# Half of the low parts of 38 weight blocks formed by POOL instead of DVE

## The chip, the cores and the metric

The kernel runs on one core of a Trainium2 chip. The time is device microseconds of one launch: the median of the runs, which are compared with the runs of the kernel before on the same chip.

## What is computed

A model of two blocks of two layers each, 256 tokens of width 1024, all in 32-bit floats. The change lies in the first block, whose layer has a differential attention, an attention over the 64 best keys of an index score (the sparse attention), gates, and 32 experts:

```python
h = x @ w_in
dq, dkk, dv, sq, sk, sv, iq, ik, iw, ga, gb = jnp.split(h, points, axis=-1)
...
lam = jnp.exp(jnp.sum(lp[0] * lp[1])) - jnp.exp(jnp.sum(lp[2] * lp[3])) + lam_init
ya = diff_attention(dq, dkk, dv, lam)
ya = (rms_norm(ya, subln_g) * (1.0 - lam_init)).reshape(B, S, DIFF_WIDTH)
...
topk = min(TOPK_MAX, S // 4)
yb = dsa_attention(sq, sk, sv, iq, ik, iw, topk)
merged = jax.nn.sigmoid(ga) * (ya @ w_bd) + jax.nn.sigmoid(gb) * (yb @ w_bs)
return merged @ w_o
```

The second block (latent attention, block attention, retention, a squared-ReLU MLP) and the experts stay as they are.

## The kernel before

**Split products.** A dense product is made of three matmuls on high and low parts (`mm3`, line 1149): high by high, high by low, low by high. So each dense weight block, up to 128 x 2048 words, 1 MB, is split after it has landed in a ring buffer: ACT rounds it into the high part `WSh` in two halves (line 2126, signal `hi_done`, one count for each half), and DVE subtracts high from the landed block into the low part `WSl`, again in two halves (line 1516, signal `lo_done`). There are 218 such blocks of different widths; 38 of them, all 2048 words wide, are touched by the change. There are three landing buffers (`RING`) and three pairs of high and low parts (`PAIRS`).

**Order.** A planner (`Plan`) writes one list of steps, and each of the engines walks the same list and does its part of each step, in that order. PE, ACT, DVE, POOL and SP's queue are each in order; they meet only in semaphores. `take` puts the fetch and the split of a block into the list two blocks ahead of the matmuls that use it (`ahead`, line 183). The split of block i+3 may begin when PE has read block i, since it goes into the same pair; the fetch of block i+3 waits in SP's queue until the split of block i is done (line 1126).

**The stretch of the change.** In layer 0 it begins behind the iq projections. In the list stand: the small late loads that POOL issues (line 2380 and on, among them the tokens `X`), the rotary tables on DVE, POOL's scaling of `X` by a constant (line 2389, behind the landing of `X`), the rotary step of iq. Then come the four blocks of the sq and sk projections (blocks 4 to 7), the index scores, two blocks each of dq, dk and dv with the steps of the top-64 search between them (DVE, lines 1647 to 1657), the transposes, the differential attention with one gate block in each of its waits, and the sparse attention with sv, the branch product and two more gate blocks among its steps. A round of softmax goes PE (scores), DVE (mask and row maximum, lines 1670 to 1674), ACT (exponentials, line 2182), DVE (lines 1681 to 1698), PE (transposes of the probabilities, line 1276). In the list, the split of a block stands between those DVE steps. Layer 1 has the same stretch with no loads and no scaling in front of it.

**POOL before.** In this stretch it issues the late loads, scales `X`, and takes two tiny powers for the norm of the differential attention (line 2374, one for each half of the tokens), for which DVE waits.

Of the kernel before, what the change touches and what calls it, by code (L numbers as in the profile page):

```python
# [7 lines left out]
F32 = mybir.dt.float32  # L8
# [3 lines left out]
ALU = mybir.AluOpType  # L12
# [33 lines left out]
PAIRS = 3  # L46
# [54 lines left out]
class Plan:  # L101
# [3 lines left out]
    def __init__(self, order):  # L105
# [9 lines left out]
        self.limit = 3  # L115
        self.also = {}

    def add(self, kind, **fields):
# [71 lines left out]
    def prepare(self, j, spec):  # L190
# [7 lines left out]
        if not self.is_raw(at) and j not in self.split_no:  # L198
            m = self.split_no[j] = len(self.split_block)
            self.split_block.append(j)  # L200
            self.add("split", i=j, m=m, n=width(at), buffer=self.fetched[j])
            self.give_back(j)

# [148 lines left out]
    def first_layer(self, l):  # L352
# [11 lines left out]
        if l == 0:  # L364
            self.add("scale_x", l=l)
        self.add("rope", name="iq", l=l)
        self.columns("w_in", "sq", l, W1["sq"], 1024, src)
        if l == 0:
# [28 lines left out]
        def diff_out():  # L397
# [3 lines left out]
            self.todo.extend(self.gates("w_in", l, "gb", W1["gb"], src))  # L401
        self.attend("dsa", l, 8, (1, 2, 1), diff_out, pre=1)
        for n, name in enumerate(("A0", "A1")):
            self.lend(name, ("pe", "turned", "DT", l, 3), at=RING + n)
# [341 lines left out]
def build(nc, plan, table, wts, rows, cols, consts, pos, x0, x0T, pT, out):  # L746

    ctx = ExitStack()
    with ctx:
# [7 lines left out]
        done = {"pe": pe_done, "act": act_done, "dve": dve_done, "pool": pool_done}  # L757
        hi_done, lo_done = signal("hi_done"), signal("lo_done")
        landed = {n: signal(f"landed_{n}", 16) for n in (*(f"ring{i}" for i in range(RING)), "PT", "H", "V0", "V1", "YA", "YB", "A0", "A1", "SC", "W0", "W1")}
# [357 lines left out]
        def sync_program(e):  # L1117
            sp = Waiter(e)
            e.dma_start(XR[:, 4:8, :], x0T[:, 4:8, :]).then_inc(*xt_in[1].inc(("all",)))
            for s in plan.steps:  # L1120
                l = s.l
                if s.kind == "fetch":
                    if isinstance(s.before, tuple):
                        sp.wait_ge(done[s.before[0]], *s.before[1:])
                    elif s.before in plan.split_no:
                        sp.wait_ge(lo_done, "block", s.before)
                    elif s.before is not None:
                        sp.wait_ge(pe_done, "read", s.before)
# [14 lines left out]
        def tensor_program(e):  # L1143
# [17 lines left out]
            def bank_free(u):  # L1161
                if u >= 4:
                    pe.wait_ge(emptied(u - 4), "bank", u - 4)

            def scp_free(use):
                if use:
                    pe.wait_ge(freed("scp", use - 1), "scp", use - 1)
# [6 lines left out]
            for s in plan.steps:  # L1174
                l, i, u = s.l, s.i, s.u
                if s.kind == "wide":
                    lhs = MGS[s.h] if s.name == "w_out" else [x_[:, 4 * s.h:4 * s.h + 4, :] for x_ in XT]
                    w = [w_[:, 0:4 * s.n].rearrange("p (k n) -> p k n", k=4) for w_ in WS[plan.split_no[i] % PAIRS]]
                    pe.wait_ge(lo_done, "block", i)
                    for t in range(T):  # L1180
# [11 lines left out]
                elif s.kind in ("gate", "mlp_up", "ret_gate"):  # L1192
                    w = halves(i)
                    pe.wait_ge(lo_done, "block", i)
                    bank_free(u)
# [5 lines left out]
                elif s.kind == "branch":  # L1201
                    w = halves(i)
                    pe.wait_ge(lo_done, "block", i)
                    for m in range(2):
# [97 lines left out]
                elif s.kind in ("ple", "q_up"):  # L1302
                    w = halves(i)
                    pe.wait_ge(lo_done, "block", i)
                    if s.kind == "ple":
# [13 lines left out]
                elif s.kind == "kv_up":  # L1319
                    w = halves(i)  # L1320
                    pe.wait_ge(lo_done, "block", i)
                    bank_free(u)
# [109 lines left out]
                elif s.kind == "mlp_down":  # L1432
                    w = halves(i)
                    pe.wait_ge(lo_done, "block", i)
                    pe.wait_ge(dve_done, "mlp_up", l, s.q, s.c)
# [24 lines left out]
        def vector_program(e):  # L1460
# [43 lines left out]
            for s in plan.steps:  # L1504
                l, i, u, t = s.l, s.i, s.u, s.t
                if s.kind == "split":
                    hi, lo = WS[s.m % PAIRS]
                    buf = buffers[s.buffer]
                    for k in range(2):
                        c = slice(k * (s.n // 2), s.n // 2 if k == 0 else s.n)  # L1510
# [855 lines left out]
        def gpsimd_program(e):  # L2366
# [9 lines left out]
            for s in plan.steps:  # L2376
                l, t = s.l, s.t
                if s.kind == "late_loads":
                    pool.wait_ge(act_done, "iq", 0, 1)
# [118 lines left out]
```

## Time and profile before

| | |
|---|---|
| median of 3 runs | 1873.83 us (1873.68 to 1877.28) |
| the profiled execution | 1872.17 us |
| its span, first to last instruction | 1870.1 us |
| PE busy | 1795.5 us (96%) |
| DVE busy | 1116.6 us (60%) |
| ACT busy | 833.7 us (45%) |
| POOL busy | 69.6 us (4%) |
| stretch of the change in layer 0 | about 30 to 165 us |
| stretch of the change in layer 1 | about 510 to 650 us |

All times of rows are microseconds from the start of the span of the profiled execution. PE's busy time counts the instructions in flight, so the idle time before an instruction (in square brackets in the order-of-time view, with the instruction that ended it) tells more than a share of busy time. In the view of stretches, the number behind POOL's is the granted TensorE clock: 1.00 is 2.4 GHz, 0.50 is 1.2 GHz, a value between is a mean of the two over the stretch.

### The profile page before, as it was taken

What the parts mean: (1) busy time and instruction counts of PE and PEld (TensorE: products, weight loads), DVE (VectorE), ACT (ScalarE), POOL (GpSimd) and SP (SyncE); (2) the same over time, 40 slices, a digit from 0 to 9 for tenths busy, and PEclk for the clock granted to TensorE, in tenths of its full rate; (3) what the DMA queues carried; (4) which work ended last, traced back from release to release, by engine and by line L of the source; (5) the groups of instructions that cost most, each with busy time, mean ns of one, the idle gap of its engine ahead of it and who ended that gap; (6) DMA issues with size and microseconds to landing.
All of it is one profiled execution on the core that took longest, in us unless ns stands there. A gap on an engine that the chain in (4) does not pass through costs nothing.

```text
span 1870.1 us, 29654 instructions
## 1 busy us (share of the span) xinstructions
PE 1795.5 (96%) x12304; PEld 1480.8 (79%) x12304; DVE 1116.6 (60%) x2049; ACT 833.7 (45%) x1436; POOL 69.6 (4%) x76
## 2 busy tenths in 40 slices
PE   7999999999899999999989999999999999999998
PEld 6788885555678899555548899989998889989997
DVE  5876773233678867433248666774447577675445
ACT  5545442232445444323226465344445555344442
POOL 2000000000000000000001000001001000000011
PEclk9999999999999999999999999999999999999999
DMA  7426669999653385899984434445554533355552
GB/s 290 158 91 240 229 238 411 421 420 420 242 185 113 135 324 203 346 420 421 421 341 168 159 114 157 158 165 197 182 185 153 203 132 120 135 197 180 182 196 73
DMA packets 61052, 426.64 MB, mean 228 GB/s; under 512 B 6960, under 2 KB 7104, under 8 KB 11888
## 3 DMA queue, kind: packets, MB, share of 16 engines
q1 hardware_dynamic: 59760, 421.65, 59.6%
q8 instruction: 100, 1.64, 0.3%
q0 software_dynamic: 432, 1.82, 0.3%
q10 hardware_dynamic: 720, 1.19, 0.2%
q14 instruction: 40, 0.33, 0.0%
HBM read 423.59 MB, written 1.05 MB: 227 GB/s over the span
## 4 chain that ended last, share of the span: by engine, by line
PE 81%; DVE 14%; ACT 4%; issue 1%; POOL 1%; DMA 0%; DVEq 0%; ACTq 0%; POOLq 0%
PE bank L1147 63%; PE scp L1147 14%; DVE WSl L1516 4%; ACT SC L2182 1%; PE bank L1390 1%; DVE sm L1672 1%; ACT WSh L2126 1%; PE bank L1249 1%; PE bank L1276 1%; DVE scp L1670 1%; POOL sm L2374 1%; PE bank L1223 1%; DVE sm L1473 0%; DVE XTl L1781 0%; DVE SC L1684 0%
## 5 line engine op out<-in xcount | busy, mean ns | idle before, releaser
L1516 DVE TENSOR_TENSOR WSl<-ring,WSh 128x1024 fp32r<-128x1024 f32 (+3 forms) x404 | 459.7, 1181 | 179.6 <-ACT WSh L2126 179.4
L2126 ACT CAST WSh<-ring 128x1024 fp32r<-128x1024 f32 (+3 forms) x404 | 390.2, 1020 | 157.9 <-PE scp L1147 88.0
L1147 PE MATMUL bank<-XTh,WSh 128*128 128x256 f32 x1216 | 348.2, 286 | 4.3 <-DVE GT L1796 2.5
L1147 PE MATMUL bank<-XTl,WSh 128*128 128x256 f32 x1216 | 344.7, 283 | 0.0
L1147 PE MATMUL bank<-XTh,WSl 128*128 128x256 f32 x1216 | 344.5, 283 | 0.0
L1147 PEld LDWEIGHTS bank<-XTh,WSh 128*128 128x128 f32 x1216 | 234.0, 192 | 7.5 <-DVE WSl L1516 4.1
L1147 PEld LDWEIGHTS bank<-XTl,WSh 128*128 128x128 f32 x1216 | 234.1, 192 | 0.2
L1147 PEld LDWEIGHTS bank<-XTh,WSl 128*128 128x128 f32 x1216 | 233.9, 192 | 0.0
L1147 PE MATMUL bank<-WSh,XTh 128*128 128x512 f32 (+4 forms) x544 | 203.1, 373 | 12.4 <-DVE WSl L1516 10.7
L1147 PE MATMUL bank<-WSh,XTl 128*128 128x512 f32 (+4 forms) x544 | 201.0, 370 | 0.0
L1147 PE MATMUL bank<-WSl,XTh 128*128 128x512 f32 (+4 forms) x544 | 200.8, 369 | 0.0
L2013 DVE SCALAR_TENSOR_TENSOR TMP<-TMP,bank 128x128 f32<-128x128 f32 x64 | 18.4, 288 | 279.1 <-ACT TMP L2312 279.1
L1147 PE MATMUL scp<-WSh,FA 128*128 128x512 f32 x512 | 159.3, 389 | 0.0
L1147 PEld LDWEIGHTS bank<-WSh,XTh 128*128 128x128 f32 x544 | 104.6, 192 | 28.2 <-DVE WSl L1516 10.9
L1147 PE MATMUL bank<-FA,WSh 128*128 128x256 f32 x640 | 117.6, 286 | 0.1
L2316 ACT COPY WSF<-bank 128x256 f32<-128x256 f32 x64 | 23.8, 372 | 210.2 <-PE bank L1147 210.2
L1147 PEld LDWEIGHTS bank<-WSh,XTl 128*128 128x128 f32 x544 | 104.4, 192 | 14.1
L1147 PEld LDWEIGHTS bank<-WSl,XTh 128*128 128x128 f32 x544 | 104.7, 192 | 13.4
L1147 PEld LDWEIGHTS scp<-WSh,FA 128*128 128x128 f32 x512 | 96.1, 188 | 19.8
L1147 PEld LDWEIGHTS bank<-FA,WSh 128*128 128x128 f32 x640 | 100.5, 193 | 1.9 <-issue 1.9
L1147 PE MATMUL scp<-WSl,FA 128*128 128x512 f32 x256 | 99.7, 389 | 0.0
L1147 PE MATMUL bank<-WSh,FA 128*128 128x512 f32 (+1 forms) x336 | 94.7, 364 | 0.0
(310 smaller groups left out, 2666.9 us busy)
## 6 DMA issues: line engine op xcount, KB each, us to landing
ring<-wts SPq DMA_DIRECT2D x222, 1024.0 KB, 4.8
A<-wts SPq DMA_DIRECT2D x64, 1024.0 KB, 14.2
V<-wts SPq DMA_DIRECT2D x30, 1024.0 KB, 15.5
WSF<-wts SPq DMA_DIRECT2D x24, 1024.0 KB, 16.0
SC<-wts SPq DMA_DIRECT2D x16, 1024.0 KB, 15.5
PT<-wts SPq DMA_DIRECT2D x14, 1024.0 KB, 16.5
H<-wts SPq DMA_DIRECT2D x12, 1024.0 KB, 16.0
ring<-wts SPq DMA_DIRECT2D x8, 584.0 KB, 5.3
```

The costliest lines, as they stand in the source:

```text
L1147: return nc.tensor.matmul(dst, lhsT, rhs, start=start, stop=stop)
L1223: last = nc.tensor.transpose(bank[u % 4][0:s.w, j * P:(j + 1) * P], src, ident)
L1249: last = nc.tensor.transpose(bank[u % 4][:, j * P:(j + 1) * P], src(t, c), ident)
L1276: last = nc.tensor.transpose(bank[u % 4][:, (j - s.first) * P:(j - s.first + 1) * P], p_at(j // nk)[:, j % nk * P:(j % nk + 1) * P], ident)
L1390: last = nc.tensor.transpose(bank[u % 4][:, f * P:(f + 1) * P], SE[s.e % 2][:, f * P:(f + 1) * P], ident)
L1516: nc.vector.tensor_tensor(lo[:, c], buf[:, c], hi[:, c].bitcast(F32), ALU.subtract).then_inc(*lo_done.inc(("block", i)))
L1670: nc.vector.tensor_tensor(v, v, mask.unsqueeze(1).broadcast_to([P, 4, kl - m0]), ALU.add).then_inc(*dve_done.inc())
L1672: nc.vector.tensor_reduce(mx[:, h], scp[:, h, 0:kl], AX.X, ALU.max).then_inc(*dve_done.inc())
L2126: nc.scalar.copy(hi[:, c], buffers[s.buffer][:, c]).then_inc(*hi_done.inc(("half", i, k)))
L2182: ins = nc.scalar.activation(SC[:, h, 0:kl], scp[:, h, 0:kl], ACT.Exp, bias=nb[t][:, h:h + 1], scale=SCALE[s.name], accum_out=zs[t][:, h:h ...
L2316: nc.scalar.copy(SE[s.e % 2], bank[u % 4][:, 0:DE]).then_inc(*act_done.inc(("bank", u), ("SE", l, s.e)))
L2374: nc.gpsimd.tensor_tensor(var, var, const("nhalf")[:, 0:groups], ALU.pow).then_inc(*pool_done.inc(("pow", *name)))
```

## The change

The planner has a flag, `aid`, true from the sq projections to the end of the sparse attention in each layer. Blocks whose split step is written while it is true are "aided": 19 in each layer (6 to 24 in layer 0), the first of them the third sq and sk block, since its split is written when the first is taken. For an aided block DVE subtracts the first half alone; POOL waits for the second high half, and for the pair to be free, subtracts the second half, and counts on a semaphore of its own, `lo2_done`. PE, and SP's queue before it loads over the landed block, wait for both.

```diff
@@ prepare
             self.add("split", i=j, m=m, n=width(at), buffer=self.fetched[j])
+            if self.aid:
+                self.aided.add(j)
             self.give_back(j)
@@ first_layer
         self.add("rope", name="iq", l=l)
+        self.aid = True
         self.columns("w_in", "sq", l, W1["sq"], 1024, src)
...
         self.attend("dsa", l, 8, (1, 2, 1), diff_out, pre=1)
+        self.aid = False
@@ SP
                         sp.wait_ge(lo_done, "block", s.before)
+                        if s.before in plan.aided:
+                            sp.wait_ge(lo2_done, "block", s.before)
@@ PE
+            def split_ready(i):
+                pe.wait_ge(lo_done, "block", i)
+                if i in plan.aided:
+                    pe.wait_ge(lo2_done, "block", i)
...
-                    pe.wait_ge(lo_done, "block", i)
+                    split_ready(i)
@@ DVE
-                    for k in range(2):
+                    for k in range(1 if i in plan.aided else 2):
@@ POOL
             for s in plan.steps:
                 l, t = s.l, s.t
-                if s.kind == "late_loads":
+                if s.kind == "split" and s.i in plan.aided:
+                    hi, lo = WS[s.m % PAIRS]
+                    c = slice(s.n // 2, s.n)
+                    pool.wait_ge(hi_done, "half", s.i, 1)
+                    if blocks_free(s.m) is not None:
+                        pool.wait_ge(pe_done, "read", blocks_free(s.m))
+                    nc.gpsimd.tensor_tensor(lo[:, c], buffers[s.buffer][:, c], hi[:, c].bitcast(F32), ALU.subtract).then_inc(
+                        *lo2_done.inc(("block", s.i)))
+                elif s.kind == "late_loads":
```

## Rows read from the trace of the kernel before

**Rows 1.** The page: busy us of each engine, share of the span, instructions

```profile
PE 1795.5 (96%) x12304; PEld 1480.8 (79%) x12304; DVE 1116.6 (60%) x2049; ACT 833.7 (45%) x1436; POOL 69.6 (4%) x76
```

**Rows 2.** PE in order of time, layer 0: start, us, instruction, [idle before <- who ended it]

```profile
91.50 0.36 PE L1147 MATMUL bank<-XTh,WSh 128*128 128x256 f32 x1 [0.80 <-DVE A L1715]
...
99.99 0.38 PE L1147 MATMUL scp<-A 64*128 64x128 f32 x2 [0.77 <-ACT A L2190]
...
119.02 1.07 PE L1276 MATMUL bank<-CST,SC 128*128 128x128 f32 x4 [1.82 <-DVE SC L1698]
120.58 1.11 PE L1276 MATMUL bank<-CST,SC 128*128 128x128 f32 x4 [0.49 <-DVE SC L1698]
...
146.93 0.65 PE L1276 MATMUL bank<-CST,SC 128*128 128x128 f32 x4 [2.22 <-DVE SC L1684]
...
163.41 1.25 PE L1276 MATMUL bank<-CST,SC 128*128 128x128 f32 x8 [0.57 <-DVE H L1796]
```

**Rows 3.** PE in order of time, layer 1

```profile
537.03 1.16 PE L1147 MATMUL scp<-A 64*128 64x128 f32 x16 [1.69 <-DVE A L1715]
...
583.39 1.16 PE L1147 MATMUL scp<-A 64*128 64x128 f32 x16 [0.88 <-DVE A L1715]
...
602.43 0.66 PE L1276 MATMUL bank<-CST,SC 128*128 128x128 f32 x4 [1.84 <-DVE SC L1698]
604.00 1.12 PE L1276 MATMUL bank<-CST,SC 128*128 128x128 f32 x4 [0.91 <-DVE SC L1698]
...
630.91 1.93 PE L1276 MATMUL bank<-CST,SC 128*128 128x128 f32 x8 [2.22 <-DVE SC L1684]
```

**Rows 4.** Stretches: PE, PEld, DVE, ACT, POOL busy, granted clock, DMA share, GB/s

```profile
118.00:124.00 6.00, 4.49 (x26) 4.09 (x27) 4.77 (x19) 4.00 (x6) 0.80 (x1) 0.72 0.00 0
602.00:608.00 6.00, 4.66 (x26) 4.42 (x27) 4.63 (x20) 3.62 (x6) 1.02 (x1) 0.72 0.00 0
630.00:638.00 8.00, 6.21 (x35) 5.27 (x36) 6.62 (x11) 2.38 (x9) 0.00 (x0) 0.57 0.43 144
490.00:498.00 8.00, 2.99 (x14) 3.02 (x15) 5.64 (x14) 3.09 (x5) 1.04 (x2) 0.57 0.25 81
144.00:152.00 8.00, 4.86 (x47) 3.82 (x44) 7.86 (x11) 2.75 (x9) 0.00 (x0) 1.00 0.64 246
88.00:94.00 6.00, 5.20 (x42) 4.79 (x41) 5.57 (x11) 3.66 (x5) 0.00 (x0) 1.00 0.85 311
```

**Rows 5.** DVE and ACT in order of time ahead of two of the waits

```profile
108.32 2.35 DVE L1516 TENSOR_TENSOR WSl<-ring,WSh 128x1024 fp32r<-128x1024 f32 x2
...
142.09 2.03 ACT L2126 CAST WSh<-ring 128x1024 fp32r<-128x1024 f32 x2
...
143.71 2.35 DVE L1516 TENSOR_TENSOR WSl<-ring,WSh 128x1024 fp32r<-128x1024 f32 x2
```

**Rows 6.** POOL by line, whole span: out<-in, forms, count | busy us, mean ns | idle before

```profile
L2419 POOL TENSOR_TENSOR TMP<-TMP 128x512 f32<-128x512 f32 x32 | 33.3, 1042 | 387.5 <-ACT TMP L2355 387.5
L2389 POOL TENSOR_SCALAR X<-X 128x2048 f32<-128x2048 f32 x1 | 8.9, 8852 | 8.2 <-DMA X<-x 8.2
```

**Rows 7.** The chain of waits: start, us, the matmuls of two projection blocks

```profile
53.85 11.15 PE bank L1147 x48
```

**Rows 8.** POOL, DVE and ACT in order of time around the first aided blocks

```profile
32.47 8.85 POOL L2389 TENSOR_SCALAR X<-X 128x2048 f32<-128x2048 f32 x1 [8.19 <-DMA X<-x]
...
31.46 4.62 DVE L1516 TENSOR_TENSOR WSl<-ring,WSh 128x1024 fp32r<-128x1024 f32 x4
39.05 2.75 DVE L1516 TENSOR_TENSOR WSl<-ring,WSh 128x1024 fp32r<-128x1024 f32 x2 [2.97 <-ACT WSh L2126]
...
32.10 2.00 ACT L2126 CAST WSh<-ring 128x1024 fp32r<-128x1024 f32 x2 [0.56 <-PE bank L1147]
37.49 0.60 ACT L2155 ACTIVATE A<-bank 128x512 f32<-128x512 f32 x1 [2.12 <-PE bank L1147]
```

**Rows 9.** PE in order of time at the longest idle time nearby

```profile
495.01 3.38 PE L1249 MATMUL bank<-CST,H 128*128 128x128 f32 x16 [5.24 <-ACT H L2275]
```

More of the change, by code:

```diff
@@ L116, in __init__ @@
         self.also = {}
+        self.aid, self.aided = False, set()
     def add(self, kind, **fields):
@@ L757, in build @@
         done = {"pe": pe_done, "act": act_done, "dve": dve_done, "pool": pool_done}
-        hi_done, lo_done = signal("hi_done"), signal("lo_done")
+        hi_done, lo_done, lo2_done = signal("hi_done"), signal("lo_done"), signal("lo2_done")
         landed = {n: signal(f"landed_{n}", 16) for n in (*(f"ring{i}" for i in range(RING)), "PT", "H", "V0", "V1", "YA", "YB", "A0", "A1", "SC", "W0", "W1")}
@@ L1193, in tensor_program @@
                     w = halves(i)
-                    pe.wait_ge(lo_done, "block", i)
+                    split_ready(i)
                     bank_free(u)
@@ L1202, in tensor_program @@
                     w = halves(i)
-                    pe.wait_ge(lo_done, "block", i)
+                    split_ready(i)
                     for m in range(2):
@@ L1303, in tensor_program @@
                     w = halves(i)
-                    pe.wait_ge(lo_done, "block", i)
+                    split_ready(i)
                     if s.kind == "ple":
@@ L1320, in tensor_program @@
                     w = halves(i)
-                    pe.wait_ge(lo_done, "block", i)
+                    split_ready(i)
                     bank_free(u)
@@ L1433, in tensor_program @@
                     w = halves(i)
-                    pe.wait_ge(lo_done, "block", i)
+                    split_ready(i)
                     pe.wait_ge(dve_done, "mlp_up", l, s.q, s.c)
```

## The prediction

> **What bounds the kernel now.** I read the page first. PE is busy for 96% of the span, DVE for 60%, ACT for 45%, POOL for 4% [rows 1]. So work moved from DVE to POOL pays only where PE stands idle, and that is read in the order-of-time view of PE, from its brackets. In the stretch of layer 0 PE is idle nine times between 66 and 165 us, and the longer ones end on DVE: 0.80 us on the eviction of a transpose, 1.82 and 0.49 on the last steps of a softmax, 2.22 on a normalised softmax, 0.57 on a product's eviction [rows 2]. In layer 1 it is 0.88, then 1.84 and 0.91, then 2.22 us [rows 3]. The 0.77 us before 99.99 ends on ACT [rows 2], and the 1.69 us before 537.03 ends on an eviction at the head of the stretch that no aided split stands before [rows 3]. The whole prize in idle time is thus under 10 us of 1872.
>
> A second prize stands in the view of stretches. Behind some of these waits the granted clock falls to 1.2 GHz: 0.72 as the mean of 118 to 124 us and of 602 to 608, 0.57 over 630 to 638; but behind the equal wait of 2.22 us at 146.93 it stays at 1.00 [rows 4]. With 1 minus the mean, times two, times the stretch, that is 3.4, 3.4 and 6.9 us at the lower level. Where PE works through them it loses half: less the idle time inside them 1.4, 1.6 and 3.0 us, 6.0 together.
>
> **The change part by part.**
>
> *Off DVE.* 19 halves a layer, 38 in all. A pair of 128x1024 subtractions takes 2.35 or 2.36 us where neither is held up [rows 5], so a single one some 1.2 and the second adds 1.14; 43 us leave DVE. What each wait gets of that:
> - At 91.50 and 583.39 six and eight aided splits stand ahead among the search steps, each 1.14 us less, so DVE is far ahead. Layer 0 gains its whole 0.80. In layer 1 the next late thing is ACT's eviction of the last transpose group, which costs 0.77 at the same kind of place in layer 0 [rows 2]; so it gains 0.88 - 0.77 = 0.11.
> - At 119.02 and 602.43 one split stands in the DVE chain between the two halves of the softmax (108.32 [rows 5]); the rest is mask, maximum, ACT's exponentials and the mix. Gain 1.14 in each layer, leaving 1.17 of 2.31 and 1.61 of 2.75.
> - At 146.93 and 630.91 two splits stand ahead, but DVE then waits for ACT: the high half of the second starts on ACT at 142.09 and is there at 143.1 (half of 2.03), DVE's half takes to 144.3, and reciprocal and product some 0.9 more, to 145.2 instead of 146.87 [rows 2, 5]. Gain 1.65 in each layer.
> - At 163.41 two splits stand ahead of 0.57: gain 0.57.
>
> Together 0.80 + 1.14 + 1.65 + 0.57 = 4.2 us in layer 0 and 0.11 + 1.14 + 1.65 = 2.9 in layer 1: **7.1 us**.
>
> *Clock.* The idle times behind which it fell shrink to about 0.6 us (0.7 and 0.5 at the mix; 2.22 - 1.65). The wait of 0.80 at 91.50 left it at 1.00 [rows 4]. I take the large one and one of the two small ones as gone, 3.0 + 1.6 = **4.6 us**; bounds 0 (the 1.00 behind 2.22 us shows that a wait's length alone does not decide it) and 6.0.
>
> *Onto POOL.* The nearest row is its product of two 128x512 tiles, 1042 ns [rows 6]; twice that is 2.08 us for 128x1024, and 38 of them are 79 us. PE takes 5.6 us for a block of the projections (11.15 for two [rows 7]) and the split is two blocks ahead, so in the steady run some 11 us lie over ACT's 2.0 and POOL's 2.1; only where POOL took 9 us for one would that cover be gone. SP's fetch of block i+3 waits for the later of the two parts of block i; it must land before PE has read i, which POOL's part precedes, so it keeps a block's time of cover: nothing. In POOL's queue the powers for the norm stand between splits. The split behind the first one starts at 124 us instead of when its high part is ready; DVE took it no sooner before. Nothing of POOL is due when a power is wanted: nothing, at most one subtraction, 2.08 us, in a layer.
>
> *The new wait.* POOL's first aided split (block 6) stands behind its scaling of X, which waits for X to land and runs from 32.47 to 41.32 us [rows 8]. Block 6 is due when PE ends block 5 at 37.4 (ACT evicts that product at 37.49 [rows 8]). Behind it on PE is everything; the third and fourth sq and sk blocks, the rotary step, the index scores and all of DVE's search follow from them, so this is not got back by the slack of later waits. How long it is depends on how long the scaling takes when DVE is not subtracting. In its 8.85 us DVE subtracts for 3.6 us at first and from 39.05 on, and the scaling ends while DVE still does [rows 8]; from 36.08 to 39.05 DVE is idle. Lower end: it advances only while DVE does not, needs some 3.5 to 4 us, and with two of the four halves gone (DVE free from 34.3 on: ACT's first half at 33.1 by the row of 32.10, and 1.2) ends at 38; block 6 then takes to 40.4, since DVE subtracts at 39.05 again. Stall 3.0 us. Upper end: 8.85 us is its own pace, and block 6 is ready at 43.4: 6.0 us. The lowest value I can build, no interference at all with the short pace, is 2.0. I take **3.0**: 8.85 us is 4.3 ns an element for one input, where two inputs cost 2.0 [rows 6], and the subtractions beside it are what differs. The clock may fall behind it: behind 5.24 us of idle time [rows 9] it is 0.57 over 490 to 498, with PE at work for the last 3.0 of them [rows 4], so **1.5**, bounds 0 and 1.5.
>
> *Beside each other.* Of DVE's pairs around the scaling, one took 2.75 instead of 2.36: 0.39 us paid in 8.85 us of POOL's work [rows 8], 0.09 for a POOL subtraction of 2.08. About ten of them stand in a chain that ends in a wait: **1.0 us**, bounds 0 and 3.9 (0.39 each).
>
> **Sum:** -7.1 - 4.6 + 3.0 + 1.5 + 1.0 = -6.2 us; the profiled execution took 1872.17, so 1866.0. The median stands 1.66 above that execution: **1867.7**. Its own bounds: 1862 (all clock, start 2.0, nothing paid) to 1875 (no clock, 3.0 + 1.5 + 3.9 paid).
>
> By the Trainium skill, GPSIMD Engine Reference, Engine selection, an elementwise operation with one input runs on GPSIMD "roughly" at line rate. For 2048 elements at its 1.2 GHz that is an estimate of 1.7 us, far under the 8.85 of the row, which it would put down to the subtractions beside it; by it the start would cost the 2.0 end, and the sum be -7.2.
>
> **The rivals.**
>
> *A. The scaling's own pace is 8.85 us.* For it: the row as it stands. Against: POOL's pace with two inputs. Stall 6.0: 1867.7 + 3.0 = 1870.7, within 0.2% of no change.
>
> *B. Other engines end the waits.* The round of a softmax goes through ACT's exponentials and its two halves of a high part, 2.0 us [rows 8], and one wait of layer 0 is ACT's. If the mix and the normalised softmax gain half of what I took (2.8 instead of 5.6) and no clock comes back: -4.3 + 5.5 = +1.2, 1875.0. No change that can be told.
>
> *C. POOL's subtraction holds DVE (the other side).* Place: each of DVE's operations with two inputs in SBUF, as its own halves, the mix and the rotary products, that comes while POOL reads. If it pays p for each POOL subtraction, DVE gains 1.14 - p. From p about 1.1 the idle times stay, the clock too, and the start is paid: 1878.3, slower. At the full 2.08 the six and eight splits before 91.50 and 583.39 add 0.94 each, and so do five or so behind them in each layer: 24 x 0.94 = 22, 1901. For it: nothing here but the 0.39. Against: three DVE halves started and ended at their usual 1.2 us inside the 8.85.
>
> The Trainium skill says, in SBUF — State Buffer, Who interferes with whom, that a DVE instruction with two SBUF inputs contends with a GpSimd instruction that reads SBUF, and that whichever starts first blocks the other for the whole instruction. By that, C is the outcome wherever POOL starts first. The row does not agree for a whole instruction: DVE's subtractions at 33.8 and 39.05 did not wait for the scaling to end [rows 8].
>
> **How the numbers follow.** Chances: forecast 0.42, A 0.20, B 0.18, C 0.20. A measurement of this kernel can tell about 0.2% (3.7 us) from no change, so faster means under 1870.1. Faster: nearly all of the forecast and a quarter of A, 0.46. Slower (over 1877.6): C and a little of B, 0.22. Same: 0.32. The range leaves out the strong half of C (0.1) and a tail below: 1861 to 1882.
>
> **What would show it.** POOL's subtraction at 2.1 us near idle DVE. PE's first idle time at 37.4 us, 3 us long, ended by POOL (6 for A), with the scaling of X ending near 38 (41.3 for A). The waits at the two mixes and normalised softmaxes down to about 0.6 each, those at 91.5 and 163.4 gone, the clock at 1.00 behind 630. In C, DVE's halves well over 1.2 us in the stretch. Wrong would be: PE waiting for `lo2_done` anywhere but at block 6; DVE's own durations unchanged and the idle times unchanged all the same (B).

## The result, and the profile after

The changed kernel is slower: 1896.47 us median (1895.12 to 1897.13, 4 runs) beside 1873.76 us of the kernel before (1873.61 to 1877.28, 4 runs), ratio 1.0116, 95% interval 1.0098 to 1.0133. I had predicted 1867.7 us, with a range of 1861 to 1882, and 0.22 for slower. The profiled execution took 1896.2 us, its span is 1894.1 us, 24.0 longer than before; the mean granted clock is 0.983, before 0.990. Executions of one kernel differ by themselves: those of the kernel before, over all runs of this document, took 1871.3 to 1877.5 us with a mean granted clock of 0.992 to 0.985, so what one profiled execution shows of the clock can be off by some us.

The page's busy times, to be read beside [rows 1]:

```profile
PE 1804.4 (95%) x12304; PEld 1488.1 (79%) x12304; DVE 1123.7 (59%) x2011; ACT 834.4 (44%) x1436; POOL 162.4 (9%) x114
```

DVE has lost 38 subtractions, 38 x 1.14 = 43.3 us by the prediction's own price, and yet it is busy for 7.1 us more than before, not for 1116.6 - 43.3 = 1073.3 us. Something adds 50.4 us to instructions that are themselves unchanged. That is the first thing to see in this case: it doesn't show as a wait but as duration.

POOL by line and form (busy us, mean ns of one, then the idle time before):

```profile
L2396 POOL TENSOR_TENSOR WSl<-ring,WSh 128x1024 fp32r<-128x1024 f32 x38 | 96.2, 2535 | 176.3 <-ACT WSh L2138 176.3
L2409 POOL TENSOR_SCALAR X<-X 128x2048 f32<-128x2048 f32 x1 | 5.5, 5516 | 8.1 <-DMA X<-x 8.1
```

Where nothing is in the way a subtraction takes 2.35 us on POOL, not 2.08 (98.97 below), and the mean is 2.54. The scaling of `X`, 8.85 us in [rows 6], is 5.52.

PE in order of time, the waits that answer to [rows 2] and [rows 3], and the new one at the start (columns as there):

```profile
39.93 0.77 PE L1154 MATMUL bank<-WSh,XTh 128*128 128x512 f32 x1 [2.91 <-issue]
...
100.93 0.36 PE L1154 MATMUL bank<-XTh,WSh 128*128 128x256 f32 x1 [4.55 <-DVE A L1727]
121.47 0.66 PE L1288 MATMUL bank<-CST,SC 128*128 128x128 f32 x4 [1.51 <-DVE SC L1710]
...
161.06 1.97 PE L1288 MATMUL bank<-CST,SC 128*128 128x128 f32 x8 [4.40 <-DVE SC L1696]
...
602.61 1.83 PE L1154 MATMUL scp<-A 64*128 64x128 f32 x16 [3.16 <-DVE A L1727]
652.94 1.97 PE L1288 MATMUL bank<-CST,SC 128*128 128x128 f32 x8 [4.39 <-DVE SC L1696]
```

The 0.80 us before the gate block's matmul has become 4.55, the 2.22 us before the transposes of the normalised softmax 4.40, the same one of layer 1 4.39 instead of 2.22, and the 0.88 before the scores 3.16. All of PE's waits of the layer-0 stretch are 21.0 us together (11.1 before) and those of layer 1 14.2 us (9.1 before): 15.0 more. The other 8.9 us of the 24.0 are PE busy longer (1804.4 against 1795.5) on the same 12304 instructions.

That part is the clock: it is 0.983 or 0.984 in all four executions of the change, under every one of the kernel before. Stretches of layer 0 (columns as in [rows 4]):

```profile
160.00:162.00 2.00, 0.94 (x5) 0.84 (x6) 1.78 (x3) 0.00 (x0) 0.46 (x1) 0.50 1.04 332
164.00:166.00 2.00, 2.00 (x17) 1.67 (x16) 1.93 (x4) 0.46 (x2) 0.00 (x0) 0.50 0.31 131
```

Behind the wait of 4.40 us the granted clock is 0.50, that is 1.2 GHz, through 166 us; behind the 2.22 us of the kernel before it had stayed at 1.00 [rows 4].

POOL and DVE in order of time, by pairs: a POOL subtraction, then the instructions of DVE beside it.

```profile
62.02 2.48 POOL L2396 TENSOR_TENSOR WSl<-ring,WSh 128x1024 fp32r<-128x1024 f32 x1 [10.26 <-ACT WSh L2138]
62.17 2.42 DVE L1659 TENSOR_SCALAR TMP<-PT,sm 128x128 f32<-128x128 f32 x1
...
91.37 2.50 POOL L2396 TENSOR_TENSOR WSl<-ring,WSh 128x1024 fp32r<-128x1024 f32 x1 [2.61 <-ACT WSh L2138]
90.79 0.42 DVE L1621 TENSOR_TENSOR TMP<-A,ropeb 128x256 f32<-128x256 f32 x1
91.52 2.63 DVE L1621 TENSOR_TENSOR TMP<-A,ropeb 128x256 f32<-128x256 f32 x1
...
98.97 2.35 POOL L2396 TENSOR_TENSOR WSl<-ring,WSh 128x1024 fp32r<-128x1024 f32 x1 [5.11 <-ACT WSh L2138]
99.24 0.43 DVE L1667 MAX8 sm<-TMP 128x8 f32<-128x256 f32 x1
99.78 0.41 DVE L1669 MATCH_REPLACE8 TMP<-sm,TMP 128x256 f32<-128x256 f32 x1
...
118.33 2.35 POOL L2396 TENSOR_TENSOR WSl<-ring,WSh 128x1024 fp32r<-128x1024 f32 x1 [17.01 <-ACT WSh L2138]
118.40 2.42 DVE L1710 SCALAR_TENSOR_TENSOR SC<-SC,sm 128x128 f32<-128x128 f32 x1
121.06 0.35 DVE L1710 SCALAR_TENSOR_TENSOR SC<-SC,sm 128x128 f32<-128x128 f32 x1
...
158.02 2.43 POOL L2396 TENSOR_TENSOR WSl<-ring,WSh 128x1024 fp32r<-128x1024 f32 x1 [0.90 <-ACT WSh L2138]
158.38 2.62 DVE L1696 TENSOR_TENSOR SC<-SC,sm 128x512 f32<-128x512 f32 x1
161.12 0.69 DVE L1696 TENSOR_TENSOR SC<-SC,sm 128x512 f32<-128x512 f32 x1
172.52 2.51 POOL L2396 TENSOR_TENSOR WSl<-ring,WSh 128x1024 fp32r<-128x1024 f32 x1 [12.06 <-ACT WSh L2138]
172.67 1.40 DVE L1808 SCALAR_TENSOR_TENSOR H<-GT,bank 128x512 f32<-128x512 f32 x2
```

The rotary product at 91.52 took 2.63 us where its twin at 90.79 took 0.42; it began 0.15 us behind POOL's subtraction and ended 0.28 us behind its end. The step of the mix at 118.40 took 2.42 us instead of 0.35, the product at 158.38 took 2.62 instead of 0.69, and the search's step at 62.17, which has one input in SBUF and writes to SBUF, 2.42. But MAX8 and MATCH_REPLACE8 at 99.24 and 99.78 run inside POOL's subtraction at their usual pace, and so do the two products of 172.67, one input of which is in PSUM (0.70 us each).

So one POOL subtraction costs DVE one hold to its end, if an operation of the first kinds comes while it runs. The mean over the 38 is 50.4 / 38 = 1.33 us, or 1.27 without the 2.0 us which the scaling of `X`, and no subtraction, adds (below). Matched one by one with the kernel before, 25 of DVE's instructions beside a subtraction are over 0.15 us longer, 20 of them by 1.8 to 2.2 us; the other 13 subtractions hold nothing for so long. Ahead of the wait at 100.93 it can be added up: the six subtractions before it held DVE for 2.14 (L1659 at 62.17), 1.15 (its own half at 68.60, 2.37 us), 1.82 (L1665 at 77.03, 2.05 us instead of 0.23), 2.0 (one of four steps at 79.70), 2.23 (L1663 at 86.38, 2.52 instead of 0.29) and 2.21 us (91.52): 11.6. They relieve DVE of 6 x 1.14 = 6.8; the difference of 4.8 stands beside the 3.75 by which that wait grew.

### The profile page after: what moved, and what is told of

It is laid out like the page before. It is cut to its first block, busy times and chain, and to the rows that moved or that the text cites. A ratio compares the mean times of both kernels' runs of the same rounds, so it can differ in the third digit from the quotient of the medians.

```text
span 1894.1 us, 29758 instructions
## 1 busy us (share of the span) xinstructions
PE 1804.4 (95%) x12304; PEld 1488.1 (79%) x12304; DVE 1123.7 (59%) x2011; ACT 834.4 (44%) x1436; POOL 162.4 (9%) x114
## 3 DMA queue, kind: packets, MB, share of 16 engines
q0 software_dynamic: 432, 1.82, 0.3%
## 4 chain that ended last, share of the span: by engine, by line
PE 78%; DVE 14%; ACT 4%; issue 3%; POOL 1%; DMA 0%; DVEq 0%; ACTq 0%; POOLq 0%
PE bank L1154 61%; PE scp L1154 14%; DVE WSl L1528 3%; PE bank L1402 1%; ACT SC L2194 1%; ACT WSh L2138 1%; PE bank L1288 1%; DVE TMP L1661 1%; PE bank L1261 1%; DVE sm L1684 1%; POOL WSl L2396 1%; POOL sm L2386 1%; PE bank L1235 1%; DVE SC L1696 0%; DVE TMP L1669 0%
## 5 line engine op out<-in xcount | busy, mean ns | idle before, releaser
L1528 DVE TENSOR_TENSOR WSl<-ring,WSh 128x1024 fp32r<-128x1024 f32 (+4 forms) x366 | 424.5, 1199 | 188.9 <-ACT WSh L2138 188.7
L2386 POOL TENSOR_TENSOR sm<-sm,CST 128x1 f32<-128x1 f32 (+1 forms) x30 | 22.1, 741 | 1065.5 <-DVE sm L1500 1065.5
L2396 POOL TENSOR_TENSOR WSl<-ring,WSh 128x1024 fp32r<-128x1024 f32 x38 | 96.2, 2535 | 176.3 <-ACT WSh L2138 176.3
```

The source lines that it names most:

```text
L1528: nc.vector.tensor_tensor(lo[:, c], buf[:, c], hi[:, c].bitcast(F32), ALU.subtract).then_inc(*lo_done.inc(("block", i)))
L2386: nc.gpsimd.tensor_tensor(var, var, const("nhalf")[:, 0:groups], ALU.pow).then_inc(*pool_done.inc(("pow", *name)))
L2396: nc.gpsimd.tensor_tensor(lo[:, c], buffers[s.buffer][:, c], hi[:, c].bitcast(F32), ALU.subtract).then_inc(*lo2_done.inc(("block", s.i)))
```

## The experiments

**Theories.** H, *holding*: a POOL operation that reads two tensors from SBUF holds any DVE operation of the kinds above until it ends; where the held operation is in a chain that ends one of PE's waits, this sets the time. R, the first rival, *the start*: the time is lost at block 6 behind the scaling of `X`, and the rest is clock. R2, *another engine or the hand-over*: the waits are set by ACT, by POOL's queue or by the later end of the second half, and DVE's longer durations are only a sign. All ratios below are to the kernel before, run on the same chip. "Held" is always DVE's busy time less (1116.6 - 1.14 x number of aided blocks). That counts what is held beside the scaling of `X` too: DVE's half beside it took 3.6 to 4.6 us instead of 1.22 in every run but the one with all blocks behind DVE's half (1.55), also where no block near it is aided; in the kernel before the half that it met was only 0.39 us longer than usual. So 2 to 3 us of each figure below are the scaling's and not the subtractions'.

### POOL writes but does not read

```diff
-                    nc.gpsimd.tensor_tensor(lo[:, c], buffers[s.buffer][:, c], hi[:, c].bitcast(F32), ALU.subtract).then_inc(
-                        *lo2_done.inc(("block", s.i)))
+                    for n_ in range(2):
+                        if n_:
+                            pool.wait_ge(pool_done)
+                        ins = nc.gpsimd.memset(lo[:, c].bitcast(F32), 0.0)
+                        ins.then_inc(*(lo2_done.inc(("block", s.i)) if n_ else pool_done.inc()))
```

> POOL does not read: instead of subtracting, it fills the same half of the low part with zeros, twice (two fills of 128x1024), behind the same waits and with the same count. Left out: the second half of the low part of the 38 aided blocks is zero, so those products lose that term. Theory H (a POOL instruction that reads SBUF holds DVE's next operation with two SBUF inputs until it ends): the fills take about 2.1 us together, DVE's own operations are back at their durations of before, DVE's busy time falls from 1123.7 to about 1116.6 - 43 = 1073 us, the waits at the mixes and softmaxes are those that the prediction forecast, 7 us less than before, and the clock comes back; only the start at block 6 stays. Time about 1868, at most 1875. Theory W (the second wait of PE and SP and POOL's later end do it, whatever POOL does): 1890 or more, with PE's idle times of the changed kernel in place.

Measured: 1871.31 us (1867.03 to 1872.95), ratio 0.998 (0.997 to 0.9989). The profiled execution, 1867.03 us, has a span of 1864.9. What this kernel leaves out is the second half of the low part of the aided blocks. The page, and from POOL, DVE and PE in order of time:

```profile
PE 1792.6 (96%) x12304; PEld 1478.3 (79%) x12304; DVE 1083.6 (58%) x2011; ACT 833.7 (45%) x1436; POOL 138.5 (7%) x152
...
32.88 3.90 DVE L1528 TENSOR_TENSOR WSl<-ring,WSh 128x1024 fp32r<-128x1024 f32 x1 [1.46 <-ACT WSh L2138]
...
60.05 1.97 POOL L2399 MEMSET WSl<- 128x1024 f32 x2 [10.77 <-ACT WSh L2138]
60.22 0.86 DVE L1659 TENSOR_SCALAR TMP<-PT,sm 128x128 f32<-128x128 f32 x1
61.12 2.68 DVE L1661 SCALAR_TENSOR_TENSOR TMP<-PT,sm,TMP 128x128 f32<-128x128 f32 x7
...
146.95 1.96 POOL L2399 MEMSET WSl<- 128x1024 f32 x2 [1.38 <-ACT WSh L2138]
147.33 0.69 DVE L1696 TENSOR_TENSOR SC<-SC,sm 128x512 f32<-128x512 f32 x1
...
39.44 0.47 PE L1154 MATMUL bank<-WSh,XTh 128*128 128x512 f32 x1 [3.25 <-DVE WSl L1528]
120.98 0.66 PE L1288 MATMUL bank<-CST,SC 128*128 128x128 f32 x4 [1.08 <-DVE SC L1710]
148.08 0.66 PE L1288 MATMUL bank<-CST,SC 128*128 128x128 f32 x4 [0.61 <-DVE SC L1696]
```

POOL is occupied for 1.97 us per block at the same places, with the same waits and signals, and the waits shrink as the prediction had them shrink: 2.22 to 0.61 (0.57 forecast), the 0.80 at 91.50 is gone, and the 1.82 is 1.08. DVE is at 1083.6, held for 10.3 us only. The two-input operations keep their own durations beside the memset (the seven of 61.12, of which the first ones lie beside it, are 2.68 us together, as at 64.63 in the changed kernel's free stretch; the product of the normalised softmax at 147.33, inside the first fill, takes 0.69 us where it took 2.62 beside a subtraction). What remains of the 10.3 us is one half of DVE beside the scaling of `X`, which still reads (3.90 us at 32.88 instead of 1.22, 2.7 us), and one-input operations from SBUF to SBUF, such as 0.86 us at 60.22 instead of 0.28. The start wait is still there, 3.25 us. The view puts it down to DVE's half, but that of block 6 ended at 31.42; it is POOL's second fill for block 6, over at 39.34, that PE goes on behind at 39.44. R2 is refuted, since every wait for POOL's part is still there (POOL's work is 0.4 us shorter for a block, which has nothing to do with waits that DVE ends), and R too, since the start is paid and the loss is gone: what is taken away is POOL's *reading*, and with it 1.36% of the time, 25 us. The fill leaves out the arithmetic too; no run here separates the two, and that it is the reading rests on which of DVE's operations were held (those with SBUF inputs) and on the rule quoted below.

### POOL behind DVE's half

```diff
@@ POOL, split
+                    pool.wait_ge(lo_done, "block", s.i)
```

> POOL's subtraction also waits until DVE has finished the first half of the same block, nothing else is changed. Theory H: the hold depends on what DVE does behind its half. For the block at the mix (POOL at 118.33 in the changed kernel, in the middle of the mix) POOL now runs under the mask and row maximum, which read PSUM and one SBUF input, so the hold of 2.4 us there is gone in both layers; at the normalised softmax it stays (4.4 us of idle time). In the search it moves from one operation to another. Time 1886 to 1892. Theory W: POOL's part ends later than before, so the time goes up, 1897 or more.

Measured: 1881.05 us (1876.82 to 1884.87), ratio 1.003 (1.002 to 1.004), 5 us under the least that H expected; DVE 1099.2 us, held for 25.9. Half of the holding is gone. In order of time:

```profile
34.03 6.39 POOL L2410 TENSOR_SCALAR X<-X 128x2048 f32<-128x2048 f32 x1 [10.57 <-DMA X<-x]
...
120.40 2.36 POOL L2397 TENSOR_TENSOR WSl<-ring,WSh 128x1024 fp32r<-128x1024 f32 x1 [14.06 <-PE bank L1288]
...
156.47 2.63 DVE L1696 TENSOR_TENSOR SC<-SC,sm 128x512 f32<-128x512 f32 x1
...
159.15 1.12 PE L1288 MATMUL bank<-CST,SC 128*128 128x128 f32 x4 [2.09 <-DVE SC L1696]
```

POOL's subtraction at the mix now starts behind it, and the mix's steps take 0.35 us each; the wait there is 1.15 us. At the normalised softmax there are now two waits, 0.91 and 2.09 us, instead of one of 4.40, since its second product is still held (2.63 us). The start wait is 6.22 us in this execution, but not because POOL is behind DVE: DVE's half of block 6 was done at 31.86. `X` landed 11.1 us after its issue instead of 8.6, so the scaling began at 34.03, just behind the start of one of DVE's halves, and ended at 40.42; only then could POOL subtract. A purely later POOL can therefore be cheaper than an early one, which R2 excludes.

### Without the four blocks at the start of each layer's stretch

```diff
@@ first_layer
-        self.aid = True
         self.columns("w_in", "sq", l, W1["sq"], 1024, src)
+        self.aid = True
```

> The flag is set behind the sq and sk projections instead of ahead of them: 15 instead of 19 aided blocks in each layer, and none behind POOL's scaling of X. Theory H: only the start's share comes back, PE's 2.91 us of idle time at 39.93 and half of 3.3 us at the lower clock behind it, together 4.5 us: about 1892. A theory that the start pushes everything behind it late (the later waits are its consequence) expects most of the 22.7 us back: 1880 or less.

Measured: 1888.83 us (1887.43 to 1889.06), ratio 1.0072 (1.0056 to 1.0089), 7.6 us under the changed kernel and some 3 under what H expected; DVE 1128.8, held for 46.4 us, of which about 44 by the 30 subtractions, 1.46 each. Some 7.6 us of the 22.7 belong to the start. The other waits stand much as in the changed kernel: 5.18 us at 95.58 (4.55 there), 4.39 at 156.78 (4.40), 3.17 (3.16) and 3.56 (4.39) in layer 1. The start is worth about a third and is no explanation of the rest.

### The start alone

```diff
@@ prepare
             if self.aid:
-                self.aided.add(j)
+                if self.aid_n in (0, 1, 2, 3):
+                    self.aided.add(j)
+                self.aid_n += 1
@@ first_layer
-        self.aid = True
+        self.aid, self.aid_n = l == 0, 0
```

> Only the first four aided blocks of layer 0, as in the change, nothing else: the start by itself. The forecast's term was 3.0 us of idle time and 1.5 of clock. The changed kernel had 2.91 us of idle time, 3.3 us at the lower clock behind it and 3.4 more from 56.6 on: 2.9 + 1.7 + 1.5 = 6 us. So 1878 to 1880. If the start were swallowed later: 1874.

Measured: 1884.15 us (1881.13 to 1885.18), ratio 1.0043 (1.0028 to 1.0059): +0.43%, 8.1 us, more than was expected. PE in order of time:

```profile
40.32 0.77 PE L1156 MATMUL bank<-WSh,XTh 128*128 128x512 f32 x1 [3.93 <-issue]
```

Of the profiled execution's 8.9 us, 3.9 are this idle time and 4.4 are PE busy longer (1799.9). Of the clock, two stretches differ from the kernel before (columns as in [rows 4]):

```profile
38.00:46.00 8.00, 5.68 (x15) 4.52 (x16) 3.31 (x1) 0.90 (x1) 7.86 (x3) 0.57 0.55 173
154.00:162.00 8.00, 7.09 (x43) 6.40 (x44) 7.17 (x11) 4.58 (x18) 0.00 (x0) 0.57 0.28 118
```

The first lies right behind the start wait; with its 6.9 us at the lower clock, 2.3 of them idle, it costs about 2.3 us. The second lies behind the normalised softmax, whose wait is as long as before (2.24 us) but had left the clock at 1.00 in the trace of the kernel before. Whether the start brought that about or it is one execution against another is open. The two experiments on the start agree: 7.6 us taken away, 8.1 added.

### Four pieces in place of one

```diff
-                    nc.gpsimd.tensor_tensor(lo[:, c], buffers[s.buffer][:, c], hi[:, c].bitcast(F32), ALU.subtract).then_inc(
-                        *lo2_done.inc(("block", s.i)))
+                    for n_ in range(4):
+                        a = s.n // 2 + n_ * (s.n // 8)
+                        c = slice(a, a + s.n // 8)
+                        nc.gpsimd.tensor_tensor(lo[:, c], buffers[s.buffer][:, c], hi[:, c].bitcast(F32), ALU.subtract).then_inc(
+                            *lo2_done.inc(("block", s.i)))
```

> POOL's subtraction is issued as four instructions of 128x256 instead of one of 128x1024; the same elements, the same waits. Theory H, held by instruction: a DVE operation that comes while POOL reads waits at most for one piece, about 0.6 us, instead of up to 2.47; no single DVE operation in the stretch is longer than its own time plus 0.7; several can pay in turn, so the sum of what DVE pays falls less than by four, to about half. Time about 1880 to 1888. If the two engines shared by the element (both slower while together), the pieces change nothing: 1896.

Measured: 1882.78 us (1876.70 to 1884.56), ratio 1.0037 (1.002 to 1.0055); DVE 1104.5 us, held for 31.2. A piece takes 0.71 us at the least and up to 1.79. In order of time:

```profile
64.14 3.01 POOL L2399 TENSOR_TENSOR WSl<-ring,WSh 128x256 fp32r<-128x256 f32 x4 [9.83 <-ACT WSh L2138]
...
64.30 0.76 DVE L1659 TENSOR_SCALAR TMP<-PT,sm 128x128 f32<-128x128 f32 x1
65.09 3.77 DVE L1661 SCALAR_TENSOR_TENSOR TMP<-PT,sm,TMP 128x128 f32<-128x128 f32 x7
```

No operation of DVE is held for 2.1 us by a subtraction any more: 0.48 us on the step at 64.30, and 1.09 on seven steps together (3.77 against 2.68). The length of a hold follows the length of the POOL instruction, and DVE gets in between two of them. That is what a hold per instruction demands; an interference at a rate would have been the same for one instruction or four. It works the other way round too: behind the first of block 6's pieces DVE's half gets in, the second takes 1.69 us, the four together 3.7 instead of 2.34, and the start wait is 5.42 us instead of 2.91. The gain of the pieces is what is left beside that.

### Later, and with fewer blocks

Three more vary what is aided and when. The start left out *and* POOL behind DVE's half:

```diff
@@ first_layer
-        self.aid = True
         self.columns("w_in", "sq", l, W1["sq"], 1024, src)
+        self.aid = True
@@ POOL, split
+                    pool.wait_ge(lo_done, "block", s.i)
```

> Both at once: the flag set behind the sq and sk projections (15 aided blocks in each layer) and POOL behind DVE's first half. Theory H with the start as a cost of its own, counted beside the hold: what the start costs where POOL waits for DVE is PE's 6.22 us of idle time at 42.8 and half of the low clock behind it, some 9 us of the 1881 of POOL behind DVE with all blocks, so 1872 to 1874, no different from the kernel before. If the start is only a shift that later waits swallow, it stays at 1880.

Measured: 1872.51 us (1871.84 to 1874.66), ratio 0.9985 (0.9976 to 0.9995); held for 28.3 us. The waits at the normalised softmax are 1.58 and 2.09 us in layer 0, 1.49 and 2.09 in layer 1. The expectation took the start wait of 6.22 us for the price of POOL behind DVE, which it is not (above); that leaving the start out brings the ratio from 1.003 to 0.9985 shows what the start costs with POOL behind DVE, about 8 us, and not why.

Then eight blocks of each layer only, those whose POOL part, behind DVE's half, stands where DVE is idle, or reads from PSUM, or is not in a chain that PE waits for (counted from 0 in the order of their splits):

```diff
@@ prepare
             if self.aid:
-                self.aided.add(j)
+                if self.aid_n in (5, 9, 10, 11, 12, 13, 14, 17):
+                    self.aided.add(j)
+                self.aid_n += 1
@@ first_layer
-        self.aid = True
+        self.aid, self.aid_n = True, 0
@@ POOL, split
+                    pool.wait_ge(lo_done, "block", s.i)
```

> POOL behind DVE's first half, and only the eight splits of each layer behind which DVE goes on with operations that were not held in that run (maximum and replace of the search, mask and row maximum in PSUM, eviction and norm statistics, products with a PSUM input): the 6th, 10th to 15th and 18th of the nineteen. Theory H: DVE's busy time is about 1116.6 - 16 x 1.14 + at most 4 = 1102 us; the wait at 91.5 is gone in layer 0, those at the mix are down by 0.7, those at the normalised softmax by about 1.0, and one of the low stretches of the clock with them: 1866 to 1871, faster than before. If every POOL subtraction cost what the mean of the changed kernel is (1.33 us of DVE against 1.14 gained), it would be the kernel before or slower: 1874 or more.

Measured: 1871.30 us (1870.24 to 1873.96), ratio 0.9974 (0.9962 to 0.9985), just above the 1866 to 1871 that H expected; DVE 1104.0 us, held for 5.6 us, of which 2.4 beside the scaling of `X` and some 3.2 by the 16 subtractions, 0.20 each. The wait at 91.5 is gone, the one at the mix is 1.16 us, those at the normalised softmax are 2.04 us in both layers.

And the same eight with POOL not behind DVE, which is the last edit without its line on POOL:

> The same eight splits in each layer, but POOL starts as soon as the high half is there, as in the change. Theory H: at the mix POOL again starts in the middle of it and holds one of its steps for 2.4 us, and in the search some fall on products with two SBUF inputs: 4 to 8 us over the chosen eight with POOL behind DVE, 1873 to 1879. If only the choice of blocks matters and not when POOL starts, the two are equal.

Measured: 1878.17 us (1874.15 to 1878.77), ratio 1.001 (1.0001 to 1.0019); DVE 1120.2 us, held for 21.8, of which 19.5 by the 16 subtractions, 1.22 each. PE in order of time:

```profile
149.45 0.66 PE L1290 MATMUL bank<-CST,SC 128*128 128x128 f32 x4 [3.61 <-DVE SC L1698]
```

The same blocks and the same work on each engine, and leaving out one wait on POOL adds 16 us to DVE's busy time, takes the wait before the transposes from 2.04 to 3.61 us, and lengthens the kernel by 0.36%. This is the cleanest comparison for H: what differs is only *when* POOL reads.

### Past the products

The edit of the eight blocks left one gain aside: the block whose half stands on DVE just ahead of the normalised softmax, index 15. Here it is aided as well, but POOL begins it only when the two products have been made, under the operations with PSUM that follow:

```diff
@@ prepare, on the edit of the eight blocks
-                if self.aid_n in (5, 9, 10, 11, 12, 13, 14, 17):
+                if self.aid_n in (5, 9, 10, 11, 12, 13, 14, 15, 17):
                     self.aided.add(j)
+                if self.aid_n == 15:
+                    self.behind[j] = self.aid_l
@@ POOL, split
                     pool.wait_ge(lo_done, "block", s.i)
+                    if s.i in plan.behind:
+                        pool.wait_ge(dve_done, "share", "dsa", plan.behind[s.i], 0, 1)
```

> The eight chosen splits with POOL behind DVE's half, and the sixteenth of the nineteen as well, for which POOL also waits until DVE has normalised the first softmax of the sparse attention: it then falls under masks and maxima in PSUM and can't hold that product. Theory H: the wait at the normalised softmax goes from 2.04 us to about 0.9 in each layer, and the clock behind it may stay up, 2.3 to 5 us less than the eight: 1866 to 1869, ratio 0.995 to 0.997. DVE's busy time about 1102. If the hold came back at another place, DVE's busy time would rise and the time stay.

Measured: 1866.42 us (1864.98 to 1867.01, 5 runs) beside 1877.12 of the kernel before (1873.64 to 1877.43), ratio 0.9946 (0.9932 to 0.996). This is faster than the kernel before (the slowest of its five executions, 1867.01, is 6.6 us under the fastest there) and by far faster than the change. The page, and from the order of time of POOL, DVE and PE:

```profile
PE 1794.5 (96%) x12304; PEld 1479.7 (79%) x12304; DVE 1102.9 (59%) x2031; ACT 834.2 (45%) x1436; POOL 110.7 (6%) x94
...
146.07 2.35 POOL L2403 TENSOR_TENSOR WSl<-ring,WSh 128x1024 fp32r<-128x1024 f32 x1 [2.94 <-DVE SC L1700]
...
145.15 0.69 DVE L1700 TENSOR_TENSOR SC<-SC,sm 128x512 f32<-128x512 f32 x1
146.38 1.22 DVE L1686 TENSOR_TENSOR scp<-scp,TMP 128x1024 f32<-128x1024 f32 x1
...
145.08 0.66 PE L1292 MATMUL bank<-CST,SC 128*128 128x128 f32 x4 [0.88 <-DVE SC L1700]
627.70 0.66 PE L1292 MATMUL bank<-CST,SC 128*128 128x128 f32 x4 [1.48 <-DVE SC L1700]
```

POOL's subtraction lies beside the mask of the next scores, which are in PSUM, and that takes its own 1.22 us; the two waits are 0.88 and 1.48 us instead of 2.22. DVE was held for 6.8 us, of which 2.9 beside the scaling of `X` and 3.9 by the 18 subtractions, 0.22 each, against a relief of 20.5.

## Why the prediction was wrong

**The step that failed is "Beside each other".** I took the 0.39 us by which one of DVE's pairs was longer beside the scaling of `X` as a rate (0.39 in 8.85 us of POOL, 0.09 for a subtraction) and put 1.0 us into the sum, 3.9 at the most. It measured 1.27 us on the mean subtraction and 1.8 to 2.2 on each of 20 of the 38; 50.4 us in all, the scaling's 2.0 among them, which made PE's waits 15.0 us longer instead of shorter and took the clock down behind them. The row was right and the reading of it was wrong. Read again with what the runs show, [rows 8] is consistent with holds: POOL's scaling was issued at 32.47, but DVE subtracted back to back from 31.46 to 36.08. If POOL got in only then, at 36.08, and its first part lasted until DVE's pair of 39.05 could go on at 39.44, that part took 3.36 us, and DVE came 2.97 us after its start. The 0.39 is the *rest* of a hold of 3.4 us which DVE, idle by chance, missed all but the end of. The rows of the changed kernel fit with the same numbers:

```profile
31.99 5.52 POOL L2409 TENSOR_SCALAR X<-X 128x2048 f32<-128x2048 f32 x1 [8.12 <-DMA X<-x]
...
31.04 1.22 DVE L1528 TENSOR_TENSOR WSl<-ring,WSh 128x1024 fp32r<-128x1024 f32 x1
33.21 3.64 DVE L1528 TENSOR_TENSOR WSl<-ring,WSh 128x1024 fp32r<-128x1024 f32 x1 [0.95 <-ACT WSh L2138]
```

POOL can begin at 32.26, when DVE's half ends. DVE's next half comes at 33.21 and takes 3.64 us instead of 1.22, so it went on at 35.63: 3.37 us after POOL's beginning. From its end, 36.85, to POOL's, 37.51, are 0.66 us; before, DVE's first half of the pair ended at about 40.66 and the scaling at 41.32, 0.66 as well. The scaling alone would thus take some 4.0 us. The run with the start alone shows the same hold with nothing in front of it:

```profile
32.52 5.38 POOL L2411 TENSOR_SCALAR X<-X 128x2048 f32<-128x2048 f32 x1 [9.29 <-DMA X<-x]
...
32.62 4.64 DVE L1530 TENSOR_TENSOR WSl<-ring,WSh 128x1024 fp32r<-128x1024 f32 x1 [0.98 <-ACT WSh L2140]
```

DVE's half began 0.10 us behind the scaling and ended at 37.26, so it went on at 36.04, 3.52 us after POOL's start, and POOL ended 0.64 us behind it: 4.2 us for the scaling. So a one-input operation on POOL holds DVE's two-input one as a subtraction does. No run has the scaling undisturbed, and why its last part holds nobody is open.

In the prediction I set the Trainium skill's rule (SBUF — State Buffer, Who interferes with whom: of a DVE instruction with two SBUF inputs and a POOL one that reads SBUF, whichever of the two starts first blocks the other for the whole instruction) against that row, and found that the row didn't agree. The measurement decides for the rule: 2.42 us at 62.17, 2.63 at 91.52, and 0.48 only where the instruction was cut into pieces. The search step at 62.17 has one input in SBUF and was held as well, beside the memset too (0.86 us). The prediction's sentence didn't cover it, but the same section of the Trainium skill does: it counts tensor_scalar among the operations that can take the port pair shared with POOL, when their operands meet its conditions, and says that two-input operations contend with POOL's reads and not with an instruction that only writes. The memset run agrees with both: the two-input product at 147.33 keeps its 0.69 us, and beside the fills and the scaling together DVE is held for 10.3 us in all. I had also counted, as evidence against the rule, DVE halves that ran inside the bracket of POOL's 8.85 us; an instruction's bracket in the trace contains the time in which it is itself held off.

**The rival C** is what happened, and its account of the place (halves, mix, rotary products) was right, and so was its price, p = 1.1 for 1878.3 and 2.08 for 1901: the measured mean of 1.33 and time of 1896.5 lie between. A straight line between its two prices gives some 1884 for 1.33, though, 12 us less than was measured; the larger cost of the start is one part of that, and how the rest divides was not measured. It lacked the search steps with one SBUF input (62.17), and it gave the case 0.20.

**Off DVE, 7.1 us.** Right where nothing holds DVE: the memset run has 0.80 to 0, 2.31 to 1.99 (forecast 1.17), 2.22 to 0.61 and 0.57 to 0 in layer 0, and 0.88 to 0.88 (0.77), 2.75 to 2.01 (1.61) and 2.22 to 0.60 in layer 1. That is 3.3 + 2.4 = 5.7 us against 7.1; the mix was sized too high, since one half of 1.14 us gave 0.32 and 0.74; of what is missing there, 0.38 and 0.39 us are a step of the mix that the fill held (0.66 us instead of 0.28).

**Clock, -4.6 and +1.5.** In the memset run's profiled execution PE is busy for 2.9 us less than before, the forecast's net was -3.1. That execution is the fastest of ten, and the clock differs as much between executions of one kernel, so the nearness may be luck. In the change it went the other way, by 8.9.

The profiled execution of the memset run, 1867.03 us, thus stands near the 1866.0 of my sum. By the medians that kernel gained 2.4 us (3.7 by the ratio, 0.998) where the sum without its last term says 7.2: the direction of the other terms is borne out, their size only to between a third and a half.

**The start, +3.0 and +1.5.** The mechanism and the idle time were right: 2.91 us with the scaling ending at 37.5 (38 said), 3.93 in the run with the start alone, 6.22 where `X` landed later. The clock behind it was sized too low: about 2.3 us in that run right behind the wait, where I had bounded it by 1.5 from a stretch behind 5.24 us of idle time [rows 4, 9], and up to 2.1 more in a later stretch that may or may not be the start's. By the medians the start is 8 us instead of 4.5.

**Onto POOL.** 2.35 us instead of 2.08, and the cover held: PE waits for POOL's half nowhere but at block 6. **A** is wrong (the scaling ends at 37.5, its own pace is not 8.85 us). **B** is wrong: with the hold by reading gone, the waits ended by DVE shrank by 1.6 us at the normalised softmax.

**The chances.** The range of 1861 to 1882 left out the strong half of C at 0.1. It rested on one row, which had two readings; a stated rule stood for the one that I passed over. (Its own lower bound, 1873.8 - 7.1 - 6.0 + 2.0, is 1862.7 and not 1862; nothing hangs on that.)

## What to carry to other kernels

Before work goes from DVE to POOL, list what DVE does during each POOL instruction: if it is an operation whose inputs come from SBUF, count it as held to POOL's end (2.1 of 2.35 us here), and the move as a loss wherever that operation is in a chain that PE waits for. The move pays where POOL's reading is put, by a wait, under DVE's idle time or its operations with PSUM: 9 blocks a layer so placed gave -0.54%, all 19 unplaced +1.16%. And look at the *durations* of unchanged instructions first, because this kind of contention leaves an engine busy and shows no wait.

## What the runs showed of the hardware that I had not expected

- A held DVE instruction is recorded as busy: DVE's busy time rose by 7.1 us though it had 43 us less to do.
- What is held and what isn't: two SBUF inputs (0.69 becomes 2.62) and tensor_scalar from SBUF to SBUF (0.28 becomes 2.42) are; MAX8, MATCH_REPLACE8, and operations with an input in PSUM (0.70, 1.22 us beside POOL) are not.
- A POOL memset (0.96 us for 128x1024) holds no two-input operation, but still tensor_scalar from SBUF to SBUF: 0.86 us instead of 0.28.
- The price is per instruction of POOL: one of 2.35 us holds for 2.1 us, a piece of 0.71 us or more for 0.6 at most; the sum over the kernel fell from 50.4 to 31.2 us with four pieces.
- POOL's scaling with one input (128x2048, some 4.0 to 4.2 us by itself) holds DVE's next two-input half for 2.4 to 3.4 us where POOL started first. Its bracket in the trace ranges from 5.37 to 8.85 us, since that contains the time in which DVE holds it off.
- Behind the 3.93 us of idle time at the start alone the clock was 0.57 over 8 us and cost about 2.3 us. Behind the same wait of 2.2 us at the normalised softmax of layer 0 it was 1.00 in one trace [rows 4] and 0.57 in another; what decides between these stays open.
